# The experts' down products in high and low parts, with GpSimd making the low weight parts

## The chip, the cores and the metric

The program runs on one core of a Trainium2 chip. It is written by hand, engine by engine: TensorE (PE) multiplies, VectorE (DVE) and ScalarE (ACT) do the elementwise work, GpSimd (POOL) and SyncE (SP) mostly start transfers, and every dependence between engines is a semaphore. The metric is the device time of one execution in microseconds (us), less is better.

## What is computed

Two blocks of a network over 512 tokens of width 1024, all in float32: attention blocks, and in the first of them a mixture of 16 experts, which is the part that is changed.

```python
def hierarchical_moe(h, rg_w, rg_b, re_w, re_b, w_gate, w_up, w_down):
    b, s, d = h.shape
    hf = h.reshape(b * s, d)
    ...
    combine = combine.reshape(b * s, N_EXPERTS).astype(h.dtype)
    out = jnp.zeros_like(hf)
    for e in range(N_EXPERTS):
        act = jax.nn.silu(hf @ w_gate[e]) * (hf @ w_up[e])
        out = out + combine[:, e:e + 1] * (act @ w_down[e])
    return out.reshape(b, s, d)
```

`w_gate[e]` and `w_up[e]` are 1024x512, `w_down[e]` is 512x1024. Each token uses two experts.

## The kernel before

Tokens are gathered by expert, so that each of the 16 experts works on one tile of 128 rows (`P`); a loop for spare tiles stands behind them and is not entered with these inputs. `W` is 512, `KK` is 4 (128-row slices of a weight chunk), so a chunk is 128x2048 float32, 1 MB. An expert has four chunks for gate and up and two for down.

The gate and up products are made in parts. ScalarE rounds half a chunk (128x1024) to a type whose product takes TensorE one pass (the high part, `EWH`, function `expert_high`), VectorE subtracts it from the raw weights (the low part, `EWL`, function `expert_low`, both of its inputs in SBUF), and TensorE adds three one-pass products, high by high, high by low and low by high, in the generator `three`. `EWH` and `EWL` have six slots (`MOE_SLOTS`), so ScalarE may be some five half chunks ahead of TensorE. Raw chunks come through a ring of four (`RING`), which SP refills as soon as both low parts of a chunk are made. The rows of an expert are split the same way (`XSH`, `XSL`, both over the buffer `HTL`).

The down products are not made in parts. VectorE copies the transposed activations to `ACTT` (function `product_T`, in the tensor `NAT`), and `down` multiplies them in full float32 by the raw chunk in `DNW` (a piece of `BIG`): eight products an expert, four per half `m`. The trace lists each as two instructions. `DNW` has room for one expert; ScalarE issues the transfer of the next when the products on the old are done (`down_done`). The last expert's two down chunks come through `RING`.

What sets the order is the order in which each engine's program is written. In turn `e`, TensorE runs `gate_up_split(e)` (eight half chunks, with the activation transposes `act_T(e - 1)` after the third and the row transposes `rows_T(e + 1)` after the fifth) and then `expert_down(e - 1)`. VectorE runs low part 5 of expert e, the two halves of `result(e - 2)` (`L3177`, `L3179`, which read PSUM), low parts 6 and 7, `product_T(e - 1)` (`L3171`), low part 0 of expert e + 1, `rows_T` (`L3161`), `rows_low` (`L3184`), low parts 1 to 3, `product` (`L3167`) and low part 4. ScalarE runs the same list with its high parts, `expert` (`L1233`), `expert_rows_high` (`L1240`) and `silu` (`L1244`). GpSimd only starts two transfers a turn: rows in (`L1589`) and rows out (`L1593`).

Of the kernel before, what the change touches and what calls it, by code (L numbers as in the profile page):

```python
# [21 lines left out]
F32 = mybir.dt.float32  # L22
# [7 lines left out]
P = 128  # L30
D = 1024
# [134 lines left out]
def program(nc, a, out):  # L166
# [5 lines left out]
    def sem(name):  # L172
        return nc.alloc_semaphore(name)
# [110 lines left out]
    def slot(n, kk=KK, width=W):  # L284
        if kk == KK and width == W:
# [17 lines left out]
    fg_dve, fg_act = sem("forget_vector"), sem("forget_scalar")  # L303
    f_rows_in, f_pads = sem("forget_rows_in"), sem("pads_cleared")
    heads_high, heads_low = sem("head_operands_high"), sem("head_operands_low")
    fq_ready = sem("fox_q_ready")
    fm_done, fm_max, fmt_done, fm_row = (sem(f"fox_max_{x}") for x in ("products", "reduced", "transposed", "row"))
    fs_done, fp_done, fpv_blk, fo_free = (sem(f"fox_{x}") for x in
                                                   ("scores", "probs", "block_used", "out_moved"))
# [14 lines left out]
        sem(f"moe_{x}") for x in ("rows_transposed", "rows_T", "gate_up", "silu", "act",  # L324
                                  "act_transposed", "act_T", "down", "y_copied"))
    half_merged = sem("half_merged")
    x_hi, x_lo = sem("moe_rows_high"), sem("moe_rows_low")

    xs_in, y_out = [sem(f"moe_rows_in{m}") for m in range(2)], [sem(f"moe_y_stored{m}") for m in range(2)]
# [47 lines left out]
    FINAL_ROW = QS[:, :, :].rearrange("p a b -> p (a b)")  # L377
    DNW = big(12288, 2, KK, W)
    expert_down_in = loaded, loaded_rest
    DOWN_IN0 = 32, 16 * REST  # L380
    HIT1 = PT[:, 0, :, :]

    def rows_banks(E):

# [154 lines left out]
    with block as blk:  # L539
# [185 lines left out]
        def row_on_all(v):  # L725

            return v.partition_broadcast(P)
# [126 lines left out]
        def _(act):  # L854
# [371 lines left out]
            act.wait_ge(row_in, ROW_NO["gate2"])  # L1226
            act.dma_start(FINAL_ROW, row_on_all(a["final_g"])).then_inc(row_in, 16)

            def expert(E, e):

# [17 lines left out]
            expert(0, 0)  # L1248
            expert_rows_high(0)

            for e in range(EXPERTS):
# [12 lines left out]
                expert(e + 1, (e + 1) % 2)  # L1264
                if e + 1 < EXPERTS:
                    expert_rows_high(e + 1)
                    for j in range(1, 4):
                        expert_high(e + 1, j)
                if e == 0:
                    act.wait_ge(sent, 16 * 2 * NT)  # L1270
                silu(e, e % 2)
                if e + 1 < EXPERTS:
                    expert_high(e + 1, 4)
            act.wait_ge(routed, 3)
            n_spare = act.value_load(TAB[0:1, 7:8], min_val=0, max_val=SPARE)
            with act.Fori(0, SPARE) as t:
# [229 lines left out]
        def _(pool):  # L1506
# [171 lines left out]
        def _(pe):  # L1678
# [556 lines left out]
            def down(E, e, weights, starts, between=None):  # L2235
                pe.wait_ge(a_ht, E + 1)

                pe.wait_ge(y_ev, E + 1)
                for m in range(2):
                    if between is not None and m == 1:  # L2240
                        between()
                    w = weights(m)
                    for k in range(KK):
                        ins = pe.matmul(PB[5 + m][:, :], ACTT[e % 2][:, k, :], w[:, k, :], start=(k == 0), stop=(k == KK - 1))  # L2244
                        if k == 0 and starts:
                            begin(ins, None)
                    ins.then_inc(down_done, 1)

            def expert_down(e, between=None):

                def chunk(m):
                    if e == EXPERTS - 1:
                        await_chunk(CH["moe"] + LAST_DOWN + m)
                        return slot(CH["moe"] + LAST_DOWN + m)
                    pe.wait_ge(expert_down_in[m], DOWN_IN0[m] + 16 * (e + 1))
                    return DNW[:, m]

                down(e, e % 2, chunk, e == EXPERTS - 1, between)

            picked_rows_T(0, HIT)  # L2260
            picked_rows_T(1, HIT1)
# [11 lines left out]
            with pe.Fori(0, SPARE) as t:  # L2273
                with pe.If(t < n_spare):
                    E = t + EXPERTS
                    pe.wait_ge(spare_in, (t + 1) * 96)
                    gate_up(E, 0, lambda m: SPW[:, m])
                    rows_T(E + 1, 0, t + EXPERTS // 2 + 1)
                    act_T(E, 0)
                    down(E, 0, lambda m: SPW[:, 4 + m], False)  # L2280


            rows_to_T(refill=True)
# [301 lines left out]
        def _(dve):  # L2585
# [583 lines left out]
            def product_T(E, e):  # L3169
                dve.wait_ge(a_tp, E + 1)  # L3170
                V.tensor_copy(ACTT[e % 2].rearrange("p a b -> p (a b)"), PB[4][:, :]).then_inc(a_ht, 1)  # L3171

            def result(E, e, before):
# [17 lines left out]
            for e in range(EXPERTS):  # L3191
                expert_low(e, 5)
                if e > 1:
                    result(e - 2, e % 2, (e - 2) // 2)
                expert_low(e, 6)
                expert_low(e, 7)
                if e > 0:
                    product_T(e - 1, (e - 1) % 2)
                if e + 1 < EXPERTS:
                    expert_low(e + 1, 0)  # L3200
                rows_T(e + 1, (e + 1) % 2)
                if e + 1 < EXPERTS:
                    rows_low(e + 1)
                    for j in range(1, 4):
                        expert_low(e + 1, j)
                product(e, e % 2)
                if e + 1 < EXPERTS:
                    expert_low(e + 1, 4)
            product_T(EXPERTS - 1, 1)
# [427 lines left out]
```

## Time and profile before

| | us |
|---|---|
| median of 3 runs | 2214.78 |
| lowest and highest | 2211.32, 2216.1 |
| the profiled execution | 2210.18 |
| its span, from the first to the last instruction | 2208.6 |
| one expert's turn, from 648.53 to 667.66 | 19.13 |
| TensorE busy in that turn | 19.13 |
| VectorE busy in that turn | 14.16 |
| ScalarE busy in that turn | 11.06 |

Times in a trace are microseconds from the span's start. An instruction's row names the source line, the engine, the operation, and the tile it writes, an arrow, and the tiles it reads. Idle time in brackets is that of the engine just before the instruction, with what ended it. The experts lie between about 503 and 810 us.

### The profile page before, as it was taken

What the parts mean: (1) busy time and instruction counts of PE and PEld (TensorE: products, weight loads), DVE (VectorE), ACT (ScalarE), POOL (GpSimd) and SP (SyncE); (2) the same over time, 40 slices, a digit from 0 to 9 for tenths busy, and PEclk for the clock granted to TensorE, in tenths of its full rate; (3) what the DMA queues carried; (4) which work ended last, traced back from release to release, by engine and by line L of the source; (5) the groups of instructions that cost most, each with busy time, mean ns of one, the idle gap of its engine ahead of it and who ended that gap; (6) DMA issues with size and microseconds to landing.
All of it is one profiled execution on the core that took longest, in us unless ns stands there. A gap on an engine that the chain in (4) does not pass through costs nothing.

```text
span 2208.6 us, 25770 instructions
## 1 busy us (share of the span) xinstructions
PE 2121.1 (96%) x9980; PEld 1660.3 (75%) x9980; DVE 1212.5 (55%) x1830; ACT 951.9 (43%) x1484; POOL 185.7 (8%) x235
## 2 busy tenths in 40 slices
PE   7999999999999968999999999999999999999998
PEld 4768678877776637887778888878877767888887
DVE  6747654478777745367544454463446646445444
ACT  4455532346655524236431134343357755112343
POOL 1240001101000010000000000020223200000000
PEclk9999999999999988999999999999989999999999
DMA  9304034939999972220222222232100012222221
GB/s 396 118 27 178 7 127 162 380 129 362 383 382 383 384 266 92 93 88 18 77 96 102 98 95 96 96 106 96 64 2 2 3 50 91 101 102 93 100 96 58
DMA packets 55345, 309.31 MB, mean 140 GB/s; under 512 B 10830, under 2 KB 11603, under 8 KB 24117
## 3 DMA queue, kind: packets, MB, share of 16 engines
q1 hardware_dynamic: 36788, 230.25, 28.2%
q0 software_dynamic: 11520, 41.60, 4.8%
q10 hardware_dynamic: 6916, 35.81, 4.6%
q8 instruction: 80, 1.31, 0.2%
q14 instruction: 41, 0.34, 0.1%
HBM read 276.24 MB, written 30.99 MB: 139 GB/s over the span
## 4 chain that ended last, share of the span: by engine, by line
PE 85%; DVE 7%; ACT 4%; DMA 2%; issue 1%; POOL 0%; ACTq 0%; DVEq 0%; POOLq 0%
PE PB L1727 62%; PE PB L2244 5%; PE PB L2502 3%; DMA BIG<-in_k_caus 1%; PE PB L2476 1%; PE PB L2475 1%; PE PB L2436 1%; PE PB L1879 1%; PE PB L1900 1%; DVE WL L2641 1%; PE PB L2002 1%; PE PB L2073 1%; PE PB L2509 1%; PE PB L2192 1%; DVE X L2699 1%
## 5 line engine op out<-in xcount | busy, mean ns | idle before, releaser
L2641 DVE TENSOR_TENSOR WL<-RING,WH 128x1024 fp32r<-128x1024 f32 x228 | 281.8, 1236 | 595.4 <-ACT WH L972 386.1
L972 ACT CAST WH<-RING 128x1024 fp32r<-128x1024 f32 x228 | 239.4, 1050 | 770.1 <-PE PB L1727 764.9
L1727 PE MATMUL PB<-HTH,WH 128*128 128x512 f32 x1056 | 412.8, 391 | 5.4 <-DVE HTL L2668 3.7
L1727 PE MATMUL PB<-HTL,WH 128*128 128x512 f32 x1056 | 411.5, 390 | 0.0
L1727 PE MATMUL PB<-HTH,WL 128*128 128x512 f32 x1056 | 411.4, 390 | 0.0
L1727 PEld LDWEIGHTS PB<-HTH,WH 128*128 128x128 f32 x1056 | 198.6, 188 | 49.0 <-issue 6.1
L1727 PEld LDWEIGHTS PB<-HTH,WL 128*128 128x128 f32 x1056 | 198.6, 188 | 41.8
L1727 PEld LDWEIGHTS PB<-HTL,WH 128*128 128x128 f32 x1056 | 198.7, 188 | 40.8
L1727 PE MATMUL PB<-WH,NHH 128*128 128x512 f32 x496 | 193.2, 390 | 1.8 <-DVE NHL L2646 1.8
L1727 PE MATMUL PB<-WH,NHL 128*128 128x512 f32 x496 | 193.0, 389 | 0.0
L1727 PE MATMUL PB<-WL,NHH 128*128 128x512 f32 x496 | 193.0, 389 | 0.0
L3035 DVE TENSOR_TENSOR EWL<-RING,EWH 128x1024 fp32r<-128x1024 f32 x128 | 151.9, 1219 | 47.4 <-ACT EWH L1188 47.1
L1727 PE MATMUL PB<-EWH,HTL 128*128 128x512 f32 x512 | 166.5, 406 | 0.0
L1188 ACT CAST EWH<-RING 128x1024 fp32r<-128x1024 f32 x128 | 130.5, 1048 | 83.1 <-PE PB L1727 79.4
L1727 PEld LDWEIGHTS PB<-EWH,HTL 128*128 128x128 f32 x512 | 93.9, 188 | 23.9 <-issue 6.7
L1727 PEld LDWEIGHTS PB<-WH,NHH 128*128 128x128 f32 x496 | 93.1, 188 | 21.7 <-DVE NHL L2646 2.6
L1727 PEld LDWEIGHTS PB<-WL,NHH 128*128 128x128 f32 x496 | 93.1, 188 | 19.5
L1727 PEld LDWEIGHTS PB<-WH,NHL 128*128 128x128 f32 x496 | 93.1, 188 | 19.3
L2244 PE MATMUL PB<-BIG,NAT 128*128 128x512 f32 x240 | 105.6, 592 | 0.0
L1727 PE MATMUL PB<-WH,HTL 128*128 128x512 f32 (+1 forms) x296 | 99.6, 367 | 1.0 <-DVE BIG L3360 1.0
L1727 PE MATMUL PB<-EWL,HTL 128*128 128x512 f32 x256 | 100.1, 391 | 0.0
L2502 PE MATMUL PB<-PROB,NVA 128*128 128x512 f32 (+3 forms) x256 | 96.4, 459 | 3.2 <-ACT RST L1452 3.2
(589 smaller groups left out, 3419.7 us busy)
## 6 DMA issues: line engine op xcount, KB each, us to landing
RING<-in_mlp_w_packed SPq DMA_DIRECT2D x64, 1024.0 KB, 4.8
RING<-in_expert_w_gate_packed SPq DMA_DIRECT2D x32, 1024.0 KB, 7.4
RING<-in_expert_w_up_packed SPq DMA_DIRECT2D x32, 1024.0 KB, 11.3
BIG<-in_expert_w_down_packed ACTq DMA_DIRECT2D x30, 1024.0 KB
RING<-in_w_in_packed SPq DMA_DIRECT2D x20, 1024.0 KB, 5.0
BIG<-in_ada_packed SPq DMA_DIRECT2D x9, 2048.0 KB, 9.4
dispatch_rows<-BIG POOLq DMA_DIRECT2D x24, 512.0 KB, 18.8
RING<-in_a_w_in_packed SPq DMA_DIRECT2D x10, 1024.0 KB, 5.0
```

What stands on the lines that cost most here:

```text
L972: ins = nc.scalar.copy(split_weights(stage, q)[0], halves_of(n, q))
L1188: nc.scalar.copy(EWH[:, q % MOE_SLOTS], halves_of(CH["moe"] + GU_AT[e] + j // 2, j)).then_inc(high_ready, 1)
L1727: yield pe.matmul(dst, lhs, rhs, start=(start and n == 0), stop=(stop_ and n == 2))
L1879: ins = pe.matmul(PB[u % 4][:, 0:nk + nk % 2], lhs, rhs, start=(n == 0), stop=(n == len(pairs) - 1))
L1900: ins = pe.matmul(PB[6 + u % 2][:, 0:DH], PT[0:n, u % 2, j, :], v(it, h, b, j, n), start=(j == 0), stop=(j == len(m) - 1))
L2002: ins = pe.matmul(PB[5 + h % 2][:, j * P:T], v, PROB[:, n % 4, 0:T - j * P], start=(j == 0), stop=(j == NT - 1))
L2073: ins = pe.matmul(PB[3 + 4 * (p % 2)][half, i * P:(i + 1) * P], SV[:, j, h * DH:(h + 1) * DH], SPT[:, u % 4, j, :], start=(j == 0), stop=( ...
L2192: ins = pe.transpose(PB[d // 4][:, (d % 4) * P:(d % 4 + 1) * P], XS[e % 2][:, d * P:(d + 1) * P], IDENT[:, :])
L2244: ins = pe.matmul(PB[5 + m][:, :], ACTT[e % 2][:, k, :], w[:, k, :], start=(k == 0), stop=(k == KK - 1))
L2502: ins = pe.matmul(dst, lhs, rhs, start=(j == 0), stop=last)
L2641: return V.tensor_tensor(wl, halves_of(n, q), wh.bitcast(F32), ALU.subtract)
L3035: V.tensor_tensor(EWL[:, q % MOE_SLOTS], halves_of(CH["moe"] + GU_AT[e] + j // 2, j), EWH[:, q % MOE_SLOTS].bitcast(F32), ALU.subtract).th ...
```

## The change

The down products are made of parts too. Per expert, ScalarE makes the high part of each half of the down weights (`down_high`, a 128x2048 cast into `DNH`) and the high part of the transposed activations (`act_high`, into `ACTH`). GpSimd makes the low part of each half of the weights (a 128x2048 subtraction into `DNL`), and VectorE makes the low part of the activations (`product_low`) where it made the copy. TensorE then runs 24 products an expert through `three` in place of eight in full float32. For the last expert VectorE makes the low weight parts (`last_down_low`), in four slots of `EWH` and `EWL`. The raw down weights of the next expert are requested when GpSimd has read the old ones, and no longer when the products are done. The row of the final gain gets a place and a load time of its own, since its old buffer is used. Two semaphores are used a second time.

The core of the diff:

```diff
+            def down_high(e, m):
+                if e == EXPERTS - 1:
+                    n = CH["moe"] + LAST_DOWN + m
+                    act.wait_ge(arrived[n % SLOTS], slot_count(n))
+                    act.wait_ge(part_begun, part_no("moe", 8 * e + 4 + 2 * m) + 1)
+                else:
+                    act.wait_ge(expert_down_in[m], DOWN_IN0[m] + 16 * (e + 1))
+                    if e > 0:
+                        act.wait_ge(down_done, 2 * (e - 1) + m + 1)
+                nc.scalar.copy(down_parts(e, m)[0], down_raw(e, m)).then_inc(dn_hi, 1)
+            def next_down_weights(e, m):
+                if 0 < e < EXPERTS - 1:
+                    act.wait_ge(dn_lo, down_low_no(e - 1, m))
+                    expert_down_weights(e, m)
+            def act_high(e):
+                act.wait_ge(a_tp, e + 1)
+                nc.scalar.copy(act_parts(e)[0].rearrange("p a b -> p (a b)"), PB[4][:, :]).then_inc(dn_hi, 1)
             for e in range(EXPERTS):
+                if e > 0:
+                    down_high(e - 1, 0)
                 expert_high(e, 5)
-                if 1 < e < EXPERTS:
-                    act.wait_ge(down_done, 2 * (e - 1) - 1)
-                    expert_down_weights(e - 1, 0)
-                    act.wait_ge(down_done, 2 * (e - 1))
-                    expert_down_weights(e - 1, 1)
                 expert_high(e, 6)
+                if e > 0:
+                    down_high(e - 1, 1)
                 expert_high(e, 7)
+                if e > 0:
+                    act_high(e - 1)
                 if e + 1 < EXPERTS:
                     expert_high(e + 1, 0)
+                next_down_weights(e, 0)
...
-            for e in range(EXPERTS):
-                if e > 0:
-                    rows_in(e + 1, (e + 1) % 2, 2, disp[(e + 1) * P:(e + 2) * P, :])
+            rows_in(2, 0, 2, disp[2 * P:3 * P, :])
+            for e in range(1, EXPERTS):
+                for m in range(2):
+                    high, low = down_parts(e - 1, m)
+                    pool.wait_ge(dn_hi, down_high_no(e - 1, m))
+                    nc.gpsimd.tensor_tensor(low, down_raw(e - 1, m), high.bitcast(F32), ALU.subtract).then_inc(dn_lo, 1)
+                if e + 2 <= EXPERTS:
+                    rows_in(e + 2, e % 2, 2, disp[(e + 2) * P:(e + 3) * P, :])
                 if e > 1:
                     rows_out(e - 2, e % 2, back[(e - 2) * P:(e - 1) * P, :])
...
+            def expert_down(e, between=None):
+                pe.wait_ge(a_ht, e + 1)
+                pe.wait_ge(y_ev, e + 1)
                 for m in range(2):
                     if between is not None and m == 1:
                         between()
-                    w = weights(m)
+                    pe.wait_ge(dn_lo, down_low_no(e, m))
                     for k in range(KK):
-                        ins = pe.matmul(PB[5 + m][:, :], ACTT[e % 2][:, k, :], w[:, k, :], start=(k == 0), stop=(k == KK - 1))
-                        if k == 0 and starts:
-                            begin(ins, None)
+                        for n, ins in enumerate(three(PB[5 + m][:, :], down_parts(e, m), k, act_parts(e), k, "N", slice(0, P),
+                                                      k == 0, k == KK - 1)):
+                            if k == 0 and n == 1 and e == EXPERTS - 1:
+                                begin(ins, None)
                     ins.then_inc(down_done, 1)
...
+            def product_low(e):
+                high, low = (t.rearrange("p a b -> p (a b)") for t in act_parts(e))
+                dve.wait_ge(dn_hi, act_high_no(e))
+                V.tensor_tensor(low, PB[4][:, :], high.bitcast(F32), ALU.subtract).then_inc(a_ht, 1)
...
-                    product_T(e - 1, (e - 1) % 2)
+                    product_low(e - 1)
```

ScalarE's row of instructions over one turn of the loop, before (`L1233` the scaled rows, `L1240` their high part, `L1244` the silu, `L1219` the request of raw down weights):

```order
L1188 CAST EWH<-RING 128x1024 x3
L1244 ACTIVATE NAT<-PB 128x512
L1188 CAST EWH<-RING 128x1024 x2
L1219 DMA BIG<-in_expert_w_down_packed 128x2048 x2
L1188 CAST EWH<-RING 128x1024 x3
L1233 ACTIVATE HT<-PB,MCOLS,GS 128x128 x4
L1240 CAST HTL<-HT 128x1024
```

The same turn in the changed kernel (`L1295` is `down_high`, `L1306` is `act_high`):

```order
L1224 CAST EWH<-RING 128x1024 x3
L1278 ACTIVATE NAT<-PB 128x512
L1224 CAST EWH<-RING 128x1024
L1295 CAST DNH<-BIG 128x2048
L1224 CAST EWH<-RING 128x1024 x2
L1295 CAST DNH<-BIG 128x2048
L1224 CAST EWH<-RING 128x1024
L1306 CAST ACTH<-PB 128x512
L1224 CAST EWH<-RING 128x1024
L1255 DMA BIG<-in_expert_w_down_packed 128x2048
L1267 ACTIVATE HT<-PB,MCOLS,GS 128x128 x4
L1274 CAST HTL<-HT 128x1024
```

Two long casts and a short one are added, the first long one ahead of half chunk 5, the second between half chunks 6 and 7, and the requests are moved behind half chunk 0 of the next expert.

GpSimd in the middle of the experts, before:

```order
L1593 DMA expert_rows<-NAT 128x1024
L1589 DMA HT<-dispatch_rows 128x1024
L1593 DMA expert_rows<-NAT 128x1024
L1589 DMA HT<-dispatch_rows 128x1024
L1593 DMA expert_rows<-NAT 128x1024
```

And in the changed kernel:

```order
L1667 TENSOR_TENSOR DNL<-BIG,DNH 128x2048 x2
L1656 DMA HT<-dispatch_rows 128x1024
L1660 DMA expert_rows<-NAT 128x1024
L1667 TENSOR_TENSOR DNL<-BIG,DNH 128x2048 x2
L1656 DMA HT<-dispatch_rows 128x1024
L1660 DMA expert_rows<-NAT 128x1024
```

Ahead of each pair of transfers stand two subtractions, both of whose inputs lie in SBUF. VectorE's list keeps its order and its number of instructions until the last expert; only the copy has become a subtraction with one input in PSUM and one in SBUF.

## Rows read from the trace of the kernel before

**Rows 1.** Windows of three turns: us, busy time (instructions), clock, DMA share, GB/s.

```profile
core 0: us, PE busy (x) PEld busy (x) DVE busy (x) ACT busy (x) POOL busy (x), PEclk, DMA share, GB/s
648.53:667.66 19.13, 19.13 (x77) 13.27 (x76) 14.16 (x17) 11.06 (x14) 1.07 (x2) 1.00 0.99 384
667.66:686.79 19.13, 19.13 (x77) 13.27 (x76) 14.16 (x17) 11.04 (x14) 1.07 (x2) 1.00 0.99 382
```

**Rows 2.** Chain that ended last, within one turn: start, us, what.

```profile
642.25 6.87 PE PB L2244 x16
649.12 4.10 PE PB L1727 x18
...
661.39 3.86 PE PB L2244 x9
```

**Rows 3.** Timeline of VectorE in one turn: start, us, instruction, idle before.

```profile
650.52 1.23 DVE L3035 TENSOR_TENSOR EWL<-RING,EWH 128x1024 fp32r<-128x1024 f32 x1 [3.28 <-ACT EWH L1188]
651.67 0.68 DVE L3177 TENSOR_TENSOR NAT<-PB,ROW 128x512 f32<-128x512 f32 x1
...
652.87 2.35 DVE L3035 TENSOR_TENSOR EWL<-RING,EWH 128x1024 fp32r<-128x1024 f32 x2
655.13 0.68 DVE L3171 COPY NAT<-PB 128x512 f32<-128x512 f32 x1
...
657.33 1.37 DVE L3161 TENSOR_SCALAR HT<-PB,GS,MCOLS 128x128 f32<-128x128 f32 x4 [0.38 <-PE PB L2192]
660.01 1.23 DVE L3184 TENSOR_TENSOR HTL<-HT,HTL 128x1024 fp32r<-128x1024 f32 x1 [1.31 <-ACT HTL L1240]
```

**Rows 4.** Timeline of ScalarE in the same turn.

```profile
643.59 0.59 ACT L1244 ACTIVATE NAT<-PB 128x512 f32<-128x512 f32 x1
644.08 1.03 ACT L1188 CAST EWH<-RING 128x1024 fp32r<-128x1024 f32 x1
649.44 1.05 ACT L1188 CAST EWH<-RING 128x1024 fp32r<-128x1024 f32 x1 [4.33 <-PE PB L1727]
```

**Rows 5.** Groups by line and form, GpSimd: count, busy us, mean ns, idle before.

```profile
L1622 POOL TENSOR_TENSOR BIG<-BIG 128x2048 f32<-128x2048 f32 x1 | 4.6, 4607 | 86.8 <-ACT BIG L984 86.8
```

**Rows 6.** Timeline of VectorE around GpSimd's one 128x2048 instruction.

```profile
913.66 1.23 DVE L2641 TENSOR_TENSOR WL<-RING,WH 128x1024 fp32r<-128x1024 f32 x1 [4.21 <-ACT WH L972]
919.10 2.26 DVE L2641 TENSOR_TENSOR WL<-RING,WH 128x1024 fp32r<-128x1024 f32 x1 [4.22 <-ACT WH L972]
```

**Rows 7.** Timeline of GpSimd in that stretch and in an early one.

```profile
915.67 4.61 POOL L1622 TENSOR_TENSOR BIG<-BIG 128x2048 f32<-128x2048 f32 x1 [86.77 <-ACT BIG L984]
...
99.86 1.49 POOL L1555 CAST FQB<-FQ 64x512 fp32r<-64x512 f32 x1
...
104.04 1.50 POOL L1554 CAST FQA<-FLAGC 4x512 fp32r<-4x512 f32 x1
105.61 0.61 POOL L1555 CAST FQB<-FQ 64x512 fp32r<-64x512 f32 x1
```

**Rows 8.** Timeline of VectorE in the early stretch.

```profile
99.50 1.37 DVE L2641 TENSOR_TENSOR WL<-RING,WH 128x1024 fp32r<-128x1024 f32 x1 [0.25 <-ACT WH L972]
100.90 0.69 DVE L2844 TENSOR_TENSOR FKB<-PB,FKA 64x512 fp32r<-64x512 f32 x1
...
103.84 1.23 DVE L2641 TENSOR_TENSOR WL<-RING,WH 128x1024 fp32r<-128x1024 f32 x1
```

**Rows 9.** DMA issues: operation, count, KB each, median us from issue to landing.

```profile
RING<-in_expert_w_up_packed SPq DMA_DIRECT2D x32, 1024.0 KB, 11.3
...
HT<-dispatch_rows POOLq DMA_DIRECT2D x15, 512.0 KB, 13.2
```

**Rows 10.** Windows of 2.5 us in one turn, columns as in Rows 1.

```profile
642.50:645.00 2.50, 2.50 (x7) 1.14 (x6) 2.50 (x3) 2.50 (x4) 0.00 (x0) 1.00 1.02 426
...
655.00:657.50 2.50, 2.50 (x17) 2.17 (x16) 2.12 (x4) 0.15 (x2) 0.00 (x0) 1.00 0.98 324
```

**Rows 11.** Windows of 5 us behind the experts, same columns.

```profile
805.00:810.00 5.00, 5.00 (x13) 2.10 (x12) 0.69 (x1) 0.00 (x0) 0.00 (x0) 1.00 1.00 346
810.00:815.00 5.00, 0.56 (x2) 0.00 (x0) 0.69 (x1) 0.00 (x0) 0.53 (x1) 0.93 0.70 286
815.00:820.00 5.00, 0.00 (x0) 0.00 (x0) 0.00 (x0) 0.00 (x0) 2.69 (x3) 0.50 0.29 83
```

More of the change, by code:

```diff
@@ L381, in program, with down_high_no, act_high_no, down_low_no @@
     HIT1 = PT[:, 0, :, :]
+    assert wl_at == wh_at + 4 * 2 * 2 * W
+    DNH = nc.alloc_sbuf_tensor_at("DNH", [P, 2, KK, W], F32R, offset=wh_at)
+    DNL = nc.alloc_sbuf_tensor_at("DNL", [P, 2, KK, W], F32R, offset=score_at)
+    ACTH, ACTL = (nc.alloc_sbuf_tensor_at(n_, [P, 4, P], F32R, offset=nat_at + 4 * (D + i * DFF)) for i, n_ in
+                  enumerate(("ACTH", "ACTL")))
+    LACTH, LACTL = (nc.alloc_sbuf_tensor_at(n_, [P, 4, P], F32R, offset=htl_at + 4 * i * DFF) for i, n_ in
+                    enumerate(("LACTH", "LACTL")))
+    def down_high_no(e, m):
+        return 2 + 3 * e + m + 1
+    def act_high_no(e):
+        return 2 + 3 * e + 3
+    def down_low_no(e, m):
+        return NH1 + 2 * e + m + 1
+    def down_raw(e, m):
+        n = CH["moe"] + LAST_DOWN + m
+        return slot(n) if e == EXPERTS - 1 else DNW[:, m]
+    def down_parts(e, m):
+        if e == EXPERTS - 1:
+            at_ = (8 * e + 2 + 2 * m) % MOE_SLOTS
+            return tuple(t[:, at_:at_ + 2].rearrange("p s k n -> p (s k) n") for t in (EWH, EWL))
+        return DNH[:, m], DNL[:, m]
+    def act_parts(e):
+        return tuple(t[:, :, :] for t in ((LACTH, LACTL) if e == EXPERTS - 1 else (ACTH, ACTL)))
     def rows_banks(E):
@@ L1266, in _ @@
                     expert_rows_high(e + 1)
+                next_down_weights(e, 1)
+                if e + 1 < EXPERTS:
                     for j in range(1, 4):
                         expert_high(e + 1, j)
+                else:
+                    act.wait_ge(gu_done, e)
+                    act.dma_start(FINAL_ROW, row_on_all(a["final_g"])).then_inc(row_in, 16)
+                    for m in range(2):
+                        down_high(e, m)
                 if e == 0:
@@ L1273, in _ @@
                     expert_high(e + 1, 4)
+            act_high(EXPERTS - 1)
             act.wait_ge(routed, 3)
@@ L1593, in rows_out @@
                 pool.dma_start(dst, YN[e % 2]).then_inc(y_out[e % 2], 16)
-            for e in range(EXPERTS):
-                if e > 0:
-                    rows_in(e + 1, (e + 1) % 2, 2, disp[(e + 1) * P:(e + 2) * P, :])
+            rows_in(2, 0, 2, disp[2 * P:3 * P, :])
+            for e in range(1, EXPERTS):
+                for m in range(2):
+                    high, low = down_parts(e - 1, m)
[3 more added lines that the diff above has]
+                    rows_in(e + 2, e % 2, 2, disp[(e + 2) * P:(e + 3) * P, :])
                 if e > 1:
@@ L2233, in act_T, with down @@
                 ins.then_inc(a_tp, 1)
-            def down(E, e, weights, starts, between=None):
+            def down(E, e, weights):
                 pe.wait_ge(a_ht, E + 1)
@@ L2239, in down @@
                 for m in range(2):
-                    if between is not None and m == 1:
-                        between()
                     w = weights(m)
@@ L2244, in down @@
                         ins = pe.matmul(PB[5 + m][:, :], ACTT[e % 2][:, k, :], w[:, k, :], start=(k == 0), stop=(k == KK - 1))
-                        if k == 0 and starts:
-                            begin(ins, None)
                     ins.then_inc(down_done, 1)
             def expert_down(e, between=None):
[L2251 to L2258, printed above, removed]
+                pe.wait_ge(a_ht, e + 1)
+                pe.wait_ge(y_ev, e + 1)
+                for m in range(2):
+                    if between is not None and m == 1:
+                        between()
+                    pe.wait_ge(dn_lo, down_low_no(e, m))
+                    for k in range(KK):
+                        for n, ins in enumerate(three(PB[5 + m][:, :], down_parts(e, m), k, act_parts(e), k, "N", slice(0, P),
+                                                      k == 0, k == KK - 1)):
+                            if k == 0 and n == 1 and e == EXPERTS - 1:
+                                begin(ins, None)
+                    ins.then_inc(down_done, 1)
             picked_rows_T(0, HIT)
@@ L2279, in _ @@
                     act_T(E, 0)
-                    down(E, 0, lambda m: SPW[:, 4 + m], False)
+                    down(E, 0, lambda m: SPW[:, 4 + m])
             rows_to_T(refill=True)
@@ L3171, in product_T, with last_down_low @@
                 V.tensor_copy(ACTT[e % 2].rearrange("p a b -> p (a b)"), PB[4][:, :]).then_inc(a_ht, 1)
+            def product_low(e):
+                high, low = (t.rearrange("p a b -> p (a b)") for t in act_parts(e))
+                dve.wait_ge(dn_hi, act_high_no(e))
+                V.tensor_tensor(low, PB[4][:, :], high.bitcast(F32), ALU.subtract).then_inc(a_ht, 1)
+            def last_down_low(m):
+                high, low = down_parts(EXPERTS - 1, m)
+                dve.wait_ge(dn_hi, down_high_no(EXPERTS - 1, m))
+                if m == 0:
+                    dve.wait_ge(dn_lo, down_low_no(EXPERTS - 2, 1))
+                V.tensor_tensor(low, down_raw(EXPERTS - 1, m), high.bitcast(F32), ALU.subtract).then_inc(dn_lo, 1)
             def result(E, e, before):
@@ L3205, in _ @@
                         expert_low(e + 1, j)
+                else:
+                    for m in range(2):
+                        last_down_low(m)
                 product(e, e % 2)
```

13 lines of the change are left out of this document (7 added, 6 removed).

## The prediction

> **What bounds the kernel now.** I read first the windows over whole turns of the expert loop, then the chain that ended last, then the timelines of VectorE, ScalarE and GpSimd, and last the places where GpSimd and VectorE work at the same time.
>
> An expert's turn takes 19.13 us, the same to a hundredth from turn to turn, and TensorE is busy in all of it at a granted clock of 1.00 (2.4 GHz) [rows 1]. The chain stays on TensorE too: 16 instructions of the down products in 6.87 us, then one-pass products, 18 in 4.10 us, which is 0.228 us each [rows 2]. So the turn is TensorE's. VectorE has 14.16 us of work in it and idles for 3.28 us before low part 5, 0.38 before the scaled rows and 1.31 before the rows' low part [rows 1, 3]. ScalarE has 11.06 us of work [rows 1] and idles longest, 4.33 us, before half chunk 5, which waits until TensorE begins the next expert [rows 4]. The DMA engines are 0.98 to 0.99 busy [rows 1], so they are nearly full as well. GpSimd is almost idle, 1.07 us of 19.13 [rows 1].
>
> **What the change takes from TensorE.** Eight full products (16 instructions, 6.87 us) become 24 one-pass products: 24 x 0.228 = 5.47 us [rows 2]. That is 1.40 us less in each of 16 experts, 22.4 us in all, if nothing else sets the turn. TensorE's turn would be 19.13 - 1.40 = 17.73 us.
>
> **What it adds to ScalarE.** Two casts of 128x2048. A 128x1024 cast takes 1.05 us and a 128x512 instruction 0.59 [rows 4], so 0.46 us for 512 more columns, and 1.05 + 2 x 0.46 = 1.97 us for 2048. The bound from below is 1.05 (no dearer than half the size), from above 2 x 1.05 = 2.10. With one 128x512 cast of the activations, 0.59, ScalarE's work is 11.06 + 3.94 + 0.59 = 15.6 us, below either turn. What is queued behind: the first long cast stands ahead of half chunk 5, whose idle time of 4.33 us [rows 4] would take it in; it waits for the previous expert's first down half, which is done in the middle of that idle time. The requests of raw weights move to a later line of ScalarE's program but wait for less.
>
> **What it changes on VectorE.** The copy of 0.68 us becomes a subtraction of the same size with one input in PSUM, as the results beside it, 0.68 too [rows 3]. Its cost is nothing; only its wait now passes through ScalarE's cast, 0.59 us, with the down products still 6 us off.
>
> **What it adds to GpSimd, and what that does to VectorE.** Each turn has two subtractions of 128x2048. The one such instruction of the trace, also with two SBUF inputs, took 4.607 us [rows 5], so 9.2 us a turn. As GpSimd's own time that is nothing: 9.2 + 1.1 of 17.7. But rows show that such work shuts VectorE out. While GpSimd's instruction ran from 915.67 to 920.28, VectorE began a subtraction with two SBUF inputs at 919.10. It took 2.26 us instead of 1.23, and ended 1.08 us after GpSimd did [rows 6, 7]: it stood still until the other was done. The other way round, GpSimd's casts of this length take 0.61 us, but 1.49 and 1.50 when they begin at 99.86 and 104.04, inside VectorE's two-input instructions that end at 100.87 and 105.07 [rows 7, 8]: 0.61 plus nearly the whole overlap of 1.01 and 1.03. VectorE's instruction at 100.90, with one input in PSUM, ran beside GpSimd's cast in its usual 0.69 [rows 8]. So one instruction of the two engines at a time has what a two-input read of SBUF needs, and holds it to its end; VectorE's other work is free.
>
> Nine of VectorE's 17 instructions in a turn are of that kind: eight low parts and the rows' low part, 1.23 us alone and some 1.15 in a row (two take 2.35) [rows 3]. That is 10.4 to 11.0 us, and with GpSimd's 9.2 us it is 19.6 to 20.2 us for one shared thing. That is more than today's turn, before any bad luck in the order.
>
> The Trainium skill, page "SBUF — State Buffer", section "Who interferes with whom", gives this as a rule: a VectorE instruction with two SBUF inputs and a GpSimd instruction that reads SBUF exclude each other, the first to issue has the port pair for its whole length, and a VectorE instruction with at most one SBUF input does not contend. By that rule, the rows above agree with it, and the sum with it is the one below; without it the change gives 2193 us, the first rival.
>
> The skill's page "GPSIMD Engine Reference", section "2.1 Instruction dispatch", puts the floor of a two-input instruction near 2.5 cycles per element. At 1.2 GHz that is an estimate of 4.27 us for 2048 elements where the row says 4.61; by it the sum below would be 15 x 2 x 0.34 = 10 us less. The sum goes by the row.
>
> **The turn, laid out on VectorE.** ScalarE makes the first long cast just before half chunk 5, so GpSimd's first subtraction starts when VectorE's next work is low part 5, a two-input instruction whose high part is queued behind that cast: VectorE loses 4.6 us. Low part 5 then gets its turn, since it has waited longest. Meanwhile ScalarE has done half chunks 5 and 6 and the second long cast (1.05 + 1.05 + 1.97 = 4.1 us, less than 4.6), so GpSimd's second subtraction follows at once. VectorE's two results run beside it (2 x 0.6), the rest, 4.6 - 1.2 = 3.4 us, is lost before low part 6. The wait of 1.3 us for the rows' cast stays [rows 3]; the idle 3.28 us of today is inside the first 4.6. The turn is 14.16 + 4.6 + 3.4 + 1.3 = 23.5 us, 4.3 us more than 19.13. What is late then is low part 6, so TensorE waits before half chunk 6, some 5.8 us in each turn.
>
> Fifteen turns hold GpSimd's pair (e = 1 to 15): 15 x 4.3 = 64.5 us. In the first, TensorE still has parts in hand, and VectorE's idle 3.28 us are used once: -3.3. In the last turn VectorE makes both low parts of the down weights, 4 x 1.15 = 4.6 us, in place of five of 1.15, about even. Behind it, the last down product is 1.4 us shorter, and ScalarE's cast of 0.6 lies ahead of it: -0.8. The sum is +60.4 us. The profiled execution took 2210.18, 4.6 us below the median of the runs shown; the difference is added to the median: 2214.78 + 60.4 = **2275**.
>
> DMA is not the bound then: the 7.35 MB of a turn (384 GB/s x 19.13) at today's 384 GB/s take 19.1 of 23.5 us. The moved final-gain row, 512 KB once, is nothing in a turn that has room.
>
> **The rivals.**
>
> No shutting out, TensorE stays the bound: 16 x 1.40 less and the 0.6 of the cast, 2214.8 - 21.8 = **2193**. It would need low parts of GpSimd to run beside VectorE, against all four overlaps in rows 6 to 8, and 7.35 MB in 17.73 us, 415 GB/s. The engines reach 426 in a stretch of weights alone, but 324 with as much busy share where rows are moved [rows 10]. A variant of it: TensorE is freed, but the DMA engines, full at 0.99, hold the turn near 19.0, some 2 us gained in all: **2212**, the same as now.
>
> GpSimd goes first both times: when its first subtraction ends, the second is ready, and it may get in ahead of low part 5. Then the results are hidden by nothing: 14.16 + 9.2 + 1.3 = 24.7 us a turn, 15 x 5.5 - 4.1 = +79, **2294**. Nothing in the trace shows whose turn it is when both wait.
>
> The two pack well: GpSimd's subtractions fall where VectorE waits or reads PSUM. The floor is 20.2 us a turn, 15 x 1.1 less the 0.8 at the end: **2230**; half packed it is some 22 us and 2255. Against it speaks that VectorE has only 3.8 us of free work in a turn, of which 1.2 lies beside GpSimd.
>
> The slower case without shutting out: the raw weights come late. `DNW` holds one expert, the request now stands behind GpSimd's reading, and the first long cast of the next turn comes some 10 us after it, ahead of half chunk 5 on ScalarE. Transfers issued among others take 11.3 to 13.2 us to land [rows 9]. If they do here, ScalarE stands 1 to 3 us a turn, with everything behind it: 15 x 2.3 = 35, **2250**. It decides once the landing takes over 10 us.
>
> The clock: after the experts TensorE stops, and the windows show 1.00, then 0.93, then 0.50, its level of 1.2 GHz, with TensorE busy 0.56 of 5 us and then not at all [rows 11]. In the new turn it would rest up to some 4 us in a piece, so the level may fall there. A few us at half speed fit into the 5.8 us it has spare, so I give this no price, but it is why the range reaches above 2294.
>
> **How the numbers follow.** Laid out as above, 0.62. GpSimd first, 0.12. Packed, 0.10. Raw weights late without shutting out, 0.05. DMA holds the turn, 0.03. TensorE bound, faster, 0.08. The likeliest is 2275. The range reaches from the packed floor, 2228, to 2300, and leaves out the last two and a little of each end. A measurement of this kernel tells 0.2%, 4.4 us, from no change. By the cases: faster 0.08, same 0.04, slower 0.88.
>
> **What would show it.** In the changed kernel the turn is 23 to 24 us; many low parts of VectorE last 3 to 5 us where they lasted 1.22, one or two a turn, ending 1.1 us after GpSimd's subtraction; GpSimd's subtractions take 4.6 us or up to 1.2 more where they begin inside VectorE's; TensorE waits for `EWL` before half chunk 5 or 6; the down products of an expert take 5.5 us. I am wrong if low parts keep 1.22 us beside GpSimd's work, if GpSimd's 128x2048 takes far from 4.6, or if the longest wait of the turn is for a transfer.

## The result and the profile after

The changed kernel takes 2270.36 us (median of 4 runs, 2267.13 to 2271.68), beside 2214.85 us (4 runs) for the kernel before: a ratio of 1.0251, 95% interval 1.0233 to 1.0269. It is 55.5 us slower. The profiled execution took 2271.2 us with a span of 2269.6.

The windows over one turn of the expert loop (columns as in [rows 1]: us, busy time and instructions of each engine, granted clock, DMA share, GB/s), now from one start of GpSimd's pair to the next:

```profile
658.83:681.55 22.72, 20.93 (x91) 16.78 (x90) 20.40 (x18) 15.02 (x18) 11.29 (x4) 0.92 0.88 324
```

The turn is 22.72 us where it was 19.13 [rows 1]. TensorE is no longer busy in all of it (20.93 us here, 19.7 to 19.8 in the turns beside it), VectorE's busy time has gone from 14.16 to 20.40 us with the same list of instructions, and the DMA engines have room.

Where VectorE's six microseconds come from is seen in its timeline over that turn (start, us, instruction, idle before), the lines that answer to [rows 3]:

```profile
657.84 1.22 DVE L3107 TENSOR_TENSOR EWL<-RING,EWH 128x1024 fp32r<-128x1024 f32 x1
660.26 4.36 DVE L3107 TENSOR_TENSOR EWL<-RING,EWH 128x1024 fp32r<-128x1024 f32 x1 [1.20 <-ACT EWH L1224]
664.54 0.68 DVE L3263 TENSOR_TENSOR NAT<-PB,ROW 128x512 f32<-128x512 f32 x1
665.14 0.68 DVE L3265 TENSOR_TENSOR NAT<-PB,ROW 128x512 f32<-128x512 f32 x1
665.74 5.54 DVE L3107 TENSOR_TENSOR EWL<-RING,EWH 128x1024 fp32r<-128x1024 f32 x2
671.21 0.68 DVE L3249 TENSOR_TENSOR ACTL<-PB,ACTH 128x512 fp32r<-128x512 f32 x1
...
675.41 1.22 DVE L3270 TENSOR_TENSOR HTL<-HT,HTL 128x1024 fp32r<-128x1024 f32 x1 [1.11 <-ACT HTL L1274]
```

and in GpSimd's:

```profile
658.83 10.23 POOL L1667 TENSOR_TENSOR DNL<-BIG,DNH 128x2048 fp32r<-128x2048 f32 x2 [11.43 <-ACT DNH L1295]
669.01 0.56 POOL L1656 DMA_DIRECT2D HT<-dispatch_rows  x1
```

GpSimd works from 658.83 to 669.06. Low part 5 takes 4.36 us where it took 1.23, and low parts 6 and 7 together 5.54 where they took 2.35. The two results between them, which read PSUM, keep their 0.68. As a group, the 30 subtractions of GpSimd take from 4567 to 5574 ns, the longer ones being those that first let a low part through:

```profile
L1667 POOL TENSOR_TENSOR DNL<-BIG,DNH x30: 4567/5124/5574, 522.7 to 845.2; 128x2048 fp32r<-128x2048 f32 x30
```

The waits between 560 and 760 us (who waits for what, us in total, times, longest) put TensorE behind VectorE, where before it waited for nothing:

```profile
PE PB L1799 <- DVE EWL L3107: 20.5, 8, 3.1
```

In the turn shown that wait stands ahead of half chunk 6, as its low part is made:

```profile
670.20 0.95 PE L1799 MATMUL PB<-EWH,HTL 128*128 128x512 f32 x2 [1.79 <-DVE EWL L3107]
```

### The profile page after: what moved, and what is told of

It is laid out like the page before. It is cut to its first block, busy times and chain, and to the rows that moved or that the text cites. A ratio compares the mean times of both kernels' runs of the same rounds, so it can differ in the third digit from the quotient of the medians.

```text
span 2269.6 us, 26137 instructions
## 1 busy us (share of the span) xinstructions
PE 2133.8 (94%) x10108; PEld 1703.6 (75%) x10108; DVE 1317.0 (58%) x1832; ACT 1012.0 (45%) x1532; POOL 337.8 (15%) x265
## 4 chain that ended last, share of the span: by engine, by line
PE 73%; DVE 13%; ACT 7%; issue 5%; DMA 2%; ACTq 0%; POOL 0%; DVEq 0%; POOLq 0%
PE PB L1799 55%; DVE EWL L3107 4%; PE PB L2574 3%; ACT EWH L1224 2%; DMA BIG<-in_k_caus 1%; PE PB L2548 1%; PE PB L2547 1%; PE PB L2508 1%; PE PB L1951 1%; PE PB L1972 1%; DVE HT L3233 1%; PE PB L2074 1%; PE PB L2145 1%; DVE WL L2713 1%; PE PB L2256 1%
## 5 line engine op out<-in xcount | busy, mean ns | idle before, releaser
L3107 DVE TENSOR_TENSOR EWL<-RING,EWH 128x1024 fp32r<-128x1024 f32 x128 | 254.1, 2016 | 15.0 <-ACT EWH L1224 14.8
L1799 PE MATMUL PB<-EWH,HTL 128*128 128x512 f32 x512 | 179.8, 435 | 47.2 <-DVE EWL L3107 47.2
L1667 POOL TENSOR_TENSOR DNL<-BIG,DNH 128x2048 fp32r<-128x2048 f32 x30 | 153.1, 5124 | 165.2 <-ACT DNH L1295 165.2
L1799 PEld LDWEIGHTS PB<-EWH,HTL 128*128 128x128 f32 x512 | 103.1, 209 | 75.6 <-DVE EWL L3107 54.6
L1799 PE MATMUL PB<-EWL,HTL 128*128 128x512 f32 x256 | 109.3, 427 | 0.0
```

The lines of the kernel that those rows point to most:

```text
L1667: nc.gpsimd.tensor_tensor(low, down_raw(e - 1, m), high.bitcast(F32), ALU.subtract).then_inc(dn_lo, 1)
L1799: yield pe.matmul(dst, lhs, rhs, start=(start and n == 0), stop=(stop_ and n == 2))
L3107: V.tensor_tensor(EWL[:, q % MOE_SLOTS], halves_of(CH["moe"] + GU_AT[e] + j // 2, j), EWH[:, q % MOE_SLOTS].bitcast(F32), ALU.subtract).th ...
```

## The experiments

All are edits of the changed kernel, except the last. The texts written ahead call them e1 to e11, in the order below; the ratios are to the kernel before. The time of a turn is read from the start of the same instruction in two turns that follow each other.

**GpSimd's work cut to eight columns (e1).** The waits, the long casts and the requests stay. For experts 0 to 14 TensorE multiplies by the high weight part a second time where it used the low one, so this kernel leaves the low parts of the down weights out of the result. The edit on GpSimd's side:

```diff
-                    nc.gpsimd.tensor_tensor(low, down_raw(e - 1, m), high.bitcast(F32), ALU.subtract).then_inc(dn_lo, 1)
+                    nc.gpsimd.tensor_tensor(low[:, 0, 0:8], down_raw(e - 1, m)[:, 0, 0:8], high[:, 0, 0:8].bitcast(F32),
+                                            ALU.subtract).then_inc(dn_lo, 1)
```

> GpSimd's subtraction covers 8 columns of one slice in place of 128x2048, all waits, casts and requests as in the changed kernel; TensorE multiplies by the high part a second time in place of the low part (experts 0 to 14), so the low weight parts of the down products are left out of the result. Theory A (VectorE's two-input work is shut out while GpSimd reads): low parts 5 and 6 are back at 1.22 us, and the turn falls from 22.7 us to TensorE's 17.7, or to what the DMA engines allow, about 19.0: 2193 to 2214 us. Theory B (the longer ScalarE list or late raw weights set the new turn): the turn stays above 21.5 us, 2250 us or more.

2196.76 us, ratio to the kernel before 0.9927 (0.9905 to 0.9950). Every low part of VectorE is back at its length (ns, least, median, most):

```profile
L3108 DVE TENSOR_TENSOR EWL<-RING,EWH x128: 1211/1218/1229, 457.6 to 775.9; 128x1024 fp32r<-128x1024 f32 x128
```

In the changed kernel the longest was 5557 ns. TensorE is busy in all of the stretch below and the DMA engines move 415 GB/s, so neither ScalarE's longer list nor the raw weights cost anything once GpSimd is out of the way:

```profile
640.00:680.00 40.00, 40.00 (x190) 33.23 (x189) 33.43 (x40) 35.16 (x40) 3.24 (x8) 1.00 1.01 415
```

Theory B falls. The saving on TensorE is real too: without the contention the change would be worth 16 us (2196.76 beside 2213.14), where the prediction's first rival has 21.8.

**GpSimd busy as long, but only writing (e2).** Zeros stand in for the low parts of the down weights, which are so left out.

```diff
-                    nc.gpsimd.tensor_tensor(low, down_raw(e - 1, m), high.bitcast(F32), ALU.subtract).then_inc(dn_lo, 1)
+                    link(nc.gpsimd.memset(low.bitcast(F32), 0.0))
+                    link(nc.gpsimd.memset(low.bitcast(F32), 0.0))
+                    nc.gpsimd.memset(low[:, 0:2, :].bitcast(F32), 0.0).then_inc(dn_lo, 1)
```

> GpSimd fills the low part with zeros two and a half times per half (memsets, about 4.6 us together, which write SBUF and read none) in place of the subtraction; the low weight parts of the down products of experts 0 to 14 are so left out. GpSimd's busy time stays at some 10 us a turn. Theory A with reads as the shared thing: VectorE's low parts stay at 1.22 us, 2193 to 2215 us, as with eight columns. Theory C (any GpSimd work of that length shuts VectorE out, or GpSimd's own time is what counts): low parts of 4 to 5 us stay, about 2270 us.

2194.55 us, ratio 0.9922 (0.9895 to 0.9948). GpSimd is 116.17 us busy in 200, as in the changed kernel or more (100.48), and VectorE's low parts do not notice:

```profile
560.00:760.00 200.00, 200.00 (x949) 165.66 (x948) 159.54 (x193) 168.36 (x193) 116.17 (x91) 1.00 1.01 414
```

```profile
L3109 DVE TENSOR_TENSOR EWL<-RING,EWH x128: 1214/1218/1227, 458.2 to 774.5; 128x1024 fp32r<-128x1024 f32 x128
```

So it is not GpSimd's time, nor its writing. What the subtraction has beyond a memset is its reading of SBUF and its arithmetic; that it is the reading is argued from [rows 7], where GpSimd's casts, with one SBUF input, stood beside VectorE's two-input instructions too. No run here separates the two. The Trainium skill, page "SBUF — State Buffer", section "Who interferes with whom", has it for the reads: a VectorE instruction with two SBUF inputs contends with a GpSimd instruction that reads SBUF, and not with one that only writes it. The two runs agree, with 1218 ns beside memsets and up to 5557 ns beside subtractions.

**One half on GpSimd (e3).** The first half's subtraction is whole, the second is cut to eight columns, and TensorE multiplies as in e1.

```diff
+                    part = slice(0, KK) if m == 0 else slice(0, 1)
+                    wide = slice(0, W) if m == 0 else slice(0, 8)
```

> GpSimd's subtraction is whole for the first half of the down weights and covers 8 columns for the second; TensorE multiplies by the high part in place of the low one, which is left out. Theory A: VectorE loses some 3.7 us before low part 5 and nothing before low part 6: 14.16 + 3.7 + 0.7 + 1.1 = 19.7 us a turn, about 2224 us (2215 to 2235). Theory B: as the changed kernel, 2260 or more.

2218.96 us, ratio 1.0027 (1.0014 to 1.0040). VectorE's timeline (the turn begins again at 659.85) shows one long low part, and the pair behind the results at 2.35 us:

```profile
640.31 4.91 DVE L3110 TENSOR_TENSOR EWL<-RING,EWH 128x1024 fp32r<-128x1024 f32 x1 [0.67 <-ACT EWH L1224]
...
646.34 2.35 DVE L3110 TENSOR_TENSOR EWL<-RING,EWH 128x1024 fp32r<-128x1024 f32 x2
...
659.85 4.88 DVE L3110 TENSOR_TENSOR EWL<-RING,EWH 128x1024 fp32r<-128x1024 f32 x1 [0.67 <-ACT EWH L1224]
```

The turn is 19.54 us, for 19.7 worked out.

**The second half twice (e4).**

```diff
+                    if m == 1:
+                        link(nc.gpsimd.tensor_tensor(low, down_raw(e - 1, m), high.bitcast(F32), ALU.subtract))
```

> GpSimd makes the low part of the second half twice, one after the other. Its busy time goes from 11.3 to some 16 us of a turn of 22.7, so it stays far from full. Theory A: VectorE stands another 4.6 us before low part 6, the turn is 27.3 us, 15 x 4.6 = 69 us more, about 2339 us. If GpSimd's time is hidden: within 5 us of 2270. If VectorE gets in between the two: one low part goes between them, and the turn is some 26 us, 2320 us.

2334.67 us, ratio 1.0545 (1.0504 to 1.0585), 64.3 us more than the changed kernel, 4.3 us for each of 15 added instructions of 4.6 us. That is 4 us below the 2339 of theory A. GpSimd's own lines show a turn of 27.06 us (638.19 to 665.25):

```profile
638.19 5.39 POOL L1669 TENSOR_TENSOR DNL<-BIG,DNH 128x2048 fp32r<-128x2048 f32 x1
...
654.92 4.72 POOL L1669 TENSOR_TENSOR DNL<-BIG,DNH 128x2048 fp32r<-128x2048 f32 x1 [10.29 <-ACT DNH L1295]
659.59 5.58 POOL L1668 TENSOR_TENSOR DNL<-BIG,DNH 128x2048 fp32r<-128x2048 f32 x1
665.25 5.39 POOL L1669 TENSOR_TENSOR DNL<-BIG,DNH 128x2048 fp32r<-128x2048 f32 x1
```

GpSimd still waits 10.29 us in the turn, and yet what it is given is paid nearly in full. The second and third subtraction are 0.8 to 1.0 us longer than alone: each first lets one low part of VectorE through that had been waiting. The two take turns. So what the third alternative supposed, that a low part of VectorE gets in between, is what happened, but its price of 26 us a turn was wrong: low part 6 goes first and low part 7 stands instead (the pair takes 9.88 us for 2.35 alone), and the sum of both engines' times stays.

**The granted clock (e5).** In the changed kernel the granted clock of most whole turns is 0.85 to 0.92. Products of no use keep TensorE from resting while it waits.

```diff
+                    if j == 6 and 0 < e < EXPERTS - 1:
+                        pe.wait_ge(y_ev, e)
+                        fill(PB[5], 10)
```

> The changed kernel, with ten 128x128 products of no use on TensorE ahead of half chunk 6 of experts 1 to 14, in the 3 us in which it waits there, so that it does not rest. Theory A (VectorE's list sets the turn; the granted clock of 0.85 to 0.92 there costs nothing): the clock goes to 1.00 in all turns and the turn stays 22.7 us, within 4 us of 2270. Rival (TensorE at its lower clock is part of the turn): 0.5 to 1 us less a turn, 2255 to 2262.

2272.75 us, ratio 1.0264 (1.0247 to 1.0280), the same as the changed kernel. In windows of 40 us the clock is at 1.00 from 560 to 840 us, and 0.96 in the one ahead of them. One of the windows:

```profile
640.00:680.00 40.00, 36.23 (x184) 30.16 (x183) 36.40 (x33) 23.83 (x29) 17.08 (x8) 1.00 0.91 347
```

With the clock back at 1.00 the turn is still 22.7 us (VectorE's rows' low part at 627.21, 649.93 and 672.64). The lower clock came with TensorE's waiting, and cost nothing that the runs can tell.

**The same low parts on VectorE (e6).** GpSimd only starts transfers.

```diff
+                if e > 0:
+                    down_low(e - 1, 0)
                 expert_low(e, 5)
...
                 expert_low(e, 6)
+                if e > 0:
+                    down_low(e - 1, 1)
                 expert_low(e, 7)
```

> VectorE makes the low parts of the down weights, ahead of low part 5 and behind low part 6; GpSimd makes none. Everything else as in the changed kernel. Theory A: VectorE has 14.16 + 4.6 = 18.8 us a turn and waits for 1.1 more (the rows' cast): 19.9 us, 0.8 above the kernel before: 2226 us (2215 to 2232), 45 us below the changed kernel though the same work goes to a fuller engine. Theory B (VectorE cannot take more): 2270 or above.

2220.15 us, ratio 1.0028 (1.0017 to 1.0039), 50 us below the changed kernel with more work on the engine that sets the turn, and still 6 us above the kernel before. VectorE's lines:

```profile
638.52 2.29 DVE L3245 TENSOR_TENSOR DNL<-BIG,DNH 128x2048 fp32r<-128x2048 f32 x1
...
658.01 2.29 DVE L3245 TENSOR_TENSOR DNL<-BIG,DNH 128x2048 fp32r<-128x2048 f32 x1
```

The turn is 19.49 us, for 19.9 worked out. One half costs VectorE 2.29 us when it makes it itself and 3.1 to 4.3 when GpSimd does.

**And the rows scaled by ScalarE (e7).** As above; `expert` scales eight slices in place of four, and VectorE's `rows_T` is empty.

```diff
-                for d in range(4):
+                for d in range(8):
...
-                ins.then_inc(x_ht, 1)
+                ins.then_inc(x_ht, 2)
```

> As e6, and ScalarE scales all eight slices of the rows (4 more of 128x128, some 1.5 us more a turn on it), VectorE none (1.36 us less). Theory A: VectorE 18.8 - 1.36 = 17.4 us and the wait for the rows' cast, some 1.1 to 2 us, since ScalarE is later with it: 18.6 to 19.4 us a turn, 2206 to 2218 us. TensorE's 17.7 is below that. Theory B (ScalarE's list of 16.5 us with its waits becomes the bound): above 2226.

2200.44 us, ratio 0.9936 (0.9922 to 0.9950): below both kernels, by 14 us (0.6%) and 70 us. TensorE is busy throughout, 200 us of 200, and VectorE 192.48, with a DMA share of 1.01 at 412 GB/s:

```profile
560.00:760.00 200.00, 200.00 (x949) 165.30 (x948) 192.48 (x169) 181.29 (x235) 12.29 (x23) 1.00 1.01 412
```

Three turns take 53.4 us (the rows' low part at 639.46 and 692.84), 17.8 us each, TensorE's own 17.73. It came out below the range written ahead, 2206 to 2218: the wait for the rows' cast, put at 1.1 to 2 us a turn, is 0.48, 1.10 and 0.70 us in these three turns and none ahead of the fourth; in the others from 532 us on it is between 0.23 and 1.11.

**The rows scaled by ScalarE, low parts still on GpSimd (e8).**

> The changed kernel (GpSimd makes the low weight parts), with ScalarE scaling all eight slices of the rows as in e7. Theory A: VectorE's own list is 1.36 us shorter and it loses the same to GpSimd, while the wait for the rows' cast grows by some 0.3: the turn is 22.7 - 1.0 = 21.7 us, 2255 us (2248 to 2262). If VectorE's list did not set the turn: within 4 us of 2270.

The edit is the last one alone. 2241.66 us, ratio 1.0121 (1.0104 to 1.0137), 29 us below the changed kernel where 15 were expected, and below the range written ahead. VectorE's rows' low part has no wait ahead of it. It comes again after 20.24 us here, and after 20.83 us in the turn that follows; the two lengths alternate, 20.5 us on average:

```profile
640.29 1.21 DVE L3267 TENSOR_TENSOR HTL<-HT,HTL 128x1024 fp32r<-128x1024 f32 x1
...
660.53 1.22 DVE L3267 TENSOR_TENSOR HTL<-HT,HTL 128x1024 fp32r<-128x1024 f32 x1
...
669.40 3.59 DVE L3108 TENSOR_TENSOR EWL<-RING,EWH 128x1024 fp32r<-128x1024 f32 x1 [2.52 <-ACT EWH L1224]
```

The shorter turn is 22.72 - 1.36 - 1.11 = 20.25: both the scaling and the wait for the cast behind it are gone, since ScalarE no longer waits for VectorE there. The expectation kept the wait, and was wrong by it. In the longer turn VectorE idles 2.52 us ahead of low part 5 in place of 0.83, and gets only 1.1 us of it back in a shorter stand. That VectorE's list and what it loses set the turn fits both; in every second turn ScalarE's cast adds some 0.6 us.

**The request of raw weights later (e9).**

```diff
-                next_down_weights(e, 0)
                 if e > 0:
                     act.wait_ge(x_lo, e)
...
+                next_down_weights(e, 0)
                 next_down_weights(e, 1)
```

> The changed kernel, with the first request of raw down weights moved in ScalarE's list from ahead of the scaled rows to behind their high part, where the second stands. It is issued some 11 us later, 5.2 us before the cast that needs it, where today it is 16 us before. Theory A (the turn is VectorE's, DMA has room at 0.87): the transfers land in some 6.6 us, ScalarE's first long cast and GpSimd's subtraction start 1.5 to 3 us later; VectorE's low part 5 is later by as much, 22.7 + 1.5 to 3 us a turn, 2290 to 2315 us. If the request's place is free: within 4 us of 2270.

2290.63 us, ratio 1.0334 (1.0307 to 1.0362), 20 us above the changed kernel, at the lower end of what was expected. ScalarE now waits for the raw weights, which it did not before:

```profile
656.65 0.82 ACTq L1255 DMA_DIRECT2D BIG<-in_expert_w_down_packed  x2
...
663.26 1.91 ACT L1295 CAST DNH<-BIG 128x2048 fp32r<-128x2048 f32 x1 [1.29 <-DMA BIG<-in_expert_w_down_packed]
```

The cast begins 6.6 us after the issue, and this turn is 24.02 us (VectorE's low part 5 at 642.13 and 666.15); the others are 23.1 to 24.6. So the early refill is needed by this order of casts. Its gain against the old place was not tried alone: there the request waits for products that come after the cast that needs the weights.

**GpSimd's subtractions in quarters (e10).**

```diff
+                    for k in range(KK):
+                        ins = nc.gpsimd.tensor_tensor(low[:, k, :], down_raw(e - 1, m)[:, k, :], high[:, k, :].bitcast(F32),
+                                                      ALU.subtract)
+                    ins.then_inc(dn_lo, 1)
```

> The changed kernel, with each of GpSimd's subtractions cut into four of 128x512, so that VectorE can get in between. Theory A (one shared thing, held by one instruction at a time; its sum counts): eight pieces of some 1.28 us are 10.2 us a turn where it was 9.2; VectorE waits up to 1.28 at a time but more often; turn 22 to 23.5 us, 2260 to 2282 us. Rival (it was the length of the hold that cost, pieces slip in beside VectorE's PSUM work and waits): turn 21 us or less, 2245 us or below.

2256.17 us, ratio 1.0189 (1.0163 to 1.0215), 14 us less than whole, and a little below the range written ahead. A quarter takes 1896 ns on the mean, not 1280:

```profile
L1668 POOL TENSOR_TENSOR DNL<-BIG,DNH 128x512 fp32r<-128x512 f32 x120 | 223.3, 1896 | 82.7 <-ACT DNH L1295 82.7
```

and in VectorE's turn of 21.78 us the losses are smaller and the waits are others:

```profile
642.26 2.34 DVE L3273 TENSOR_TENSOR HTL<-HT,HTL 128x1024 fp32r<-128x1024 f32 x1 [1.12 <-ACT HTL L1274]
647.27 3.50 DVE L3110 TENSOR_TENSOR EWL<-RING,EWH 128x1024 fp32r<-128x1024 f32 x3 [2.67 <-ACT EWH L1224]
...
653.36 1.48 DVE L3110 TENSOR_TENSOR EWL<-RING,EWH 128x1024 fp32r<-128x1024 f32 x1 [0.86 <-ACT EWH L1224]
...
655.96 3.45 DVE L3110 TENSOR_TENSOR EWL<-RING,EWH 128x1024 fp32r<-128x1024 f32 x2
```

VectorE loses 0.25, 1.10, 0.49 and 1.11 us in its long instructions, 3.0 us in place of 6.3. But GpSimd, let in for one quarter at a time, is 15.0 us at its eight pieces (652.46 to 667.47) and becomes late itself: ScalarE, whose requests of raw weights wait for it, stands 62.3 us in 200 behind it (39.4 ahead of its casts, 22.9 ahead of the scaled rows), TensorE 25.1, and VectorE 34.4 behind ScalarE's casts. The cost moved to another engine; the length of the hold mattered more than the expectation said, and the sum was not the whole of it.

**The rows scaled by ScalarE in the kernel before (e11).** It separates the two parts of the faster version.

> The kernel before the change, with ScalarE scaling all eight slices of the rows, as in e7. Theory: TensorE sets the turn there, 19.13 us, so VectorE's 1.36 us less is worth nothing: 2214 us within 4. It tells whether e7's 14 us come from TensorE's shorter down products (then this is the same as before) or from the rows alone (then it is near 2200).

2217.69 us, ratio 1.0009 (0.9997 to 1.0021): no difference. TensorE sets the turn there, and 1.36 us less on VectorE are worth nothing. The 14 us of e7 come from the shorter down products. The relief of VectorE alone gives nothing, and without it the shorter products give nothing either (e6, 2220.15 us).

## Why the prediction was right

The forecast was 2275 us, 60.4 above the median; 2270.36 was measured, 55.5 above.

What was read in the rows of before held. VectorE stood still while GpSimd read, in the order laid out: its low part 5 behind GpSimd's first subtraction, then low part 5 ahead of the second, the results beside it, low part 6 behind it. The first rival (no shutting out, 2193) is what the runs with eight columns and with memsets measured, 2197 and 2195, with GpSimd's subtractions taken away: the number was right and its condition is not met in the changed kernel. That DMA would hold the turn near 19.0 was wrong as a rival: the engines move 415 GB/s and TensorE's 17.73 us is reached, though [rows 1] show a share of 0.99 at 384 GB/s. The late raw weights did not happen; they did with the request 11 us later, at 20 us. The clock fell as it might, and the run with fill products shows that it had no price. GpSimd going first both times did not happen, but the turns of the changed kernel hardly test it: ScalarE's second long cast ends at 663.41, just as GpSimd's first subtraction ends (658.83 + 4.57 = 663.40), so the second was not waiting any earlier.

```profile
661.51 1.90 ACT L1295 CAST DNH<-BIG 128x2048 fp32r<-128x2048 f32 x1
```

The run with the second half twice does test it, and there a waiting low part goes ahead of a ready subtraction. The two did not pack either: 22.72 us a turn, where packing had 20.2 to 22.

The sizes, term by term. The turn was to be 14.16 + 4.6 + 3.4 + 1.3 = 23.5 us. Measured are 14.16 + (1.20 + 3.14) + 3.19 + 1.11 = 22.8, for 22.72 between turns. The first loss is 4.34 in place of 4.6, since the last 0.2 us of low part 4 lie beside GpSimd's start; the second is 3.19 in place of 3.4, and the wait for the rows' cast 1.11 in place of the 1.3 of before. The turn is 3.59 us longer than before, and not 4.3. TensorE was to wait some 5.8 us ahead of half chunk 6. Between 560 and 760 us it waits at most 3.1 there, 1.79 in the turn shown. The turn is shorter than forecast, and slower products fill a part of the rest: the 12 of half chunks 6 and 7 take 4.45 us behind the wait (670.20 to 674.65), where 12 take 2.74 from 658.69; the granted clock of the whole turn is 0.92.

The other terms were off the other way. From the first low part 5 that meets GpSimd to the next, the kernel before takes some 16.2 us, the changed one 22.55, 6.4 more, where the sum had 4.3 - 3.3 = 1.0. The changed kernel's first turn is as long as the others; the one of before is 16.2 us and not 19.13, which the sum took for it. So no slack of 3.3 was left to be used up, and it was a term with the wrong sign. Expert 0 has no results to run beside the second subtraction either:

```profile
523.63 11.38 DVE L3107 TENSOR_TENSOR EWL<-RING,EWH 128x1024 fp32r<-128x1024 f32 x3 [1.53 <-ACT EWH L1224]
```

Three low parts, 3.49 us otherwise, take 11.38. Then come 13 turns at 3.58 (low part 5 of expert 15 begins at 784.46 before and at 841.41 after), and the last turn with the last products adds 2.4, where 3.5 was worked out. The two traces differ by 61.0 us of span: 2.5 of it lie ahead of the experts' first product (503.31 and 505.77; the experiments have it between 502.96 and 506.56, so this is scatter), 1.6 up to the first shared low part, 6.4, 46.5 and 2.4 as above, and 1.7 behind the experts. The medians differ by 55.5, since the profiled execution before was 4.6 us below its median and the one after 0.8 above.

So the mechanism was right, and a part of the number's closeness is luck. In the experts' turns the sum of 60.4 (1.0 + 55.9 + 3.5) stands against 55.3 measured: the thirteen turns were 9.4 us too dear, the last 1.1, and the first 5.4 too cheap, which hid half of it. The 5.8 us that the traces differ by outside these turns had no term.

## What to carry to other kernels

Before giving GpSimd an elementwise instruction because it is idle, count the SBUF inputs of what VectorE does at that time, and add the two engines' times: while GpSimd subtracts in SBUF and VectorE reads SBUF with two inputs, they count as one engine (22.72 us a turn here, where neither engine's own work is over 14.2). Look in the trace of before for any place where the two overlap and one instruction is longer than its group; one such line (2.26 in place of 1.23 us), with the 4.61 us of GpSimd's own instruction, gave the new turn within 0.8 us. The saving may still be had, if the work goes to VectorE and other work leaves it for ScalarE, as in e7.

## What the runs showed of the hardware that was not expected

A DMA share of 0.99 was not a bound. With the same bytes a turn, 384 GB/s at 0.99 before [rows 1] became 412 to 415 GB/s at 1.01 when TensorE's turn was 17.7 us. So the share does not tell how much more could be moved; why it stands at 0.99 with less moved was not tried. The Trainium skill, page "HBM Reference", section "Specifications (TRN2)", puts a core that streams alone at about 425 GB/s; the runs here, 415 at most over 40 us, lie just below it.

When both engines had such work queued they took turns. With whole subtractions one low part of VectorE got in between GpSimd's two (5.57 us for the second, 4.57 alone); with quarters, GpSimd's pieces, 1.25 us at the least, took 1.90 us on the mean, so that cutting its work up halved what VectorE's instructions lose and made GpSimd late instead.
